# Nine of layer 1's 24 copies of the sample caches, issued at the ends of the two layers' expert sums instead of in layer 1's front

## What is computed

```python
def layer(x, caches, lp):
    q, k, v, zb, gb, u, vc = _mixer_front(_rms(x, g_mix), w_in, q_g, k_g, cv_g)
    ...
    # the sample group also returns its caches, moved on by the 4 new rows
    kv_all = jnp.concatenate([kv_buf, kv_new], axis=1)
    ...
    new_buf = kv_all[:, -lb:]
    h = x + _merge_out(ya, yb, yc, w_out)
    y = h + _peer(_rms(h, g_ffn), pq, pk1, pk2, pu, pv)

def _peer(xn, wq, k1, k2, eu, ev):     # 8 heads, the 16 best of 16384 experts for each
    ...
    hid = gelu(einsum('nd,nhkd->nhk', xb, eu[e]))
    return einsum('nhk,nhkd->nd', g * hid, ev[e])
```

## Time and profile before

| | us |
|---|---|
| median of 3 runs | 1838.96 |
| their range | 1836.76 to 1841.14 |
| the profiled execution | 1838.76 |
| its span | 1836.3 |

### The profile page before, as it was taken

One profiled execution on the slowest core, in us unless ns is written; L12 is line 12 of the kernel. 1 busy time (PEld: TensorE's weight loads), 2 busy tenths in 40 slices (PEclk: granted clock), 3 DMA queues, 4 the chain that ended last, 5 costly groups with the idle time before them and its releaser, 6 DMA issues.

```text
span 1836.3 us, 18530 instructions
## 1 busy us (share of the span) xinstructions
PE 1564.4 (85%) x5844; PEld 841.4 (46%) x5844; DVE 1104.7 (60%) x2779; ACT 606.9 (33%) x1876; POOL 695.3 (38%) x672
## 2 busy tenths in 40 slices
PE   7999999998787887688689998999888877877776
PEld 5789745444343333233157895545433333322221
DVE  2444575777878774454535466566778678644544
ACT  2342433333344332222333334333333333322222
POOL 4020343445444444333313013435454444433341
PEclk8999999999998989999899999999989988999999
DMA  8899899999999999999979988999999999999996
GB/s 280 331 360 365 333 422 421 422 421 421 421 422 421 422 421 421 422 421 421 422 285 371 373 347 355 421 422 421 421 422 421 421 422 421 421 421 422 422 422 274
DMA packets 102490, 729.70 MB, mean 397 GB/s; under 512 B 14828, under 2 KB 15959, under 8 KB 21625
## 3 DMA queue, kind: packets, MB, share of 16 engines
q0 software_dynamic: 90112, 627.43, 82.6%
q1 hardware_dynamic: 11732, 100.48, 14.0%
q10 hardware_dynamic: 548, 0.62, 0.1%
HBM read 724.22 MB, written 48.10 MB: 421 GB/s over the span
## 4 chain that ended last, share of the span: by engine, by line
DMA 45%; PE 38%; DVE 9%; ACT 2%; issue 2%; DVEq 1%; POOL 1%; ACTq 1%; SPq 0%; POOLq 0%
DMA arena<-peer_uv,idx 24%; PE bank L1742 17%; DMA qf<-peer_uv,idx 12%; PE bank L1497 7%; DMA wring<-peer_uv,idx 4%; PE bank L1666 3%; DVE arena L1322 3%; PE bank L1706 2%; DMA yt<-peer_uv,idx 2%; DMA wring<-w_out 1%; PE bank L1492 1%; DVE qf L1322 1%; DVE wring L1322 1%; ACT diag L853 1%; POOL arena L638 1%
## 5 line engine op out<-in xcount | busy, mean ns | idle before, releaser
L1742 PE MATMUL bank<-arena,diag 128*128 128x512 f32 (+1 forms) x1416 | 679.2, 623 | 141.8 <-ACT diag L853 141.8
L638 POOL DMA_INDIRECT arena<-peer_uv,idx x378 | 414.0, 1095 | 651.0 <-PE bank L1742 498.7
L1322 DVE SCALAR_TENSOR_TENSOR arena<-arena,xn 128x1024 f32<-128x1024 f32 x378 | 458.0, 1224 | 324.6 <-DMA arena<-peer_uv,idx 323.1
L1742 PEld LDWEIGHTS bank<-arena,diag 128*128 128x128 f32 (+1 forms) x1416 | 261.6, 192 | 509.4 <-issue 287.8
L845 ACT ACTIVATE act<-hid 128x2 f32<-128x2 f32 x288 | 58.6, 204 | 907.6 <-DVE arena L1322 564.4
L853 ACT ACTIVATE diag<-ident,weight 128x128 f32<-128x128 f32 (+1 forms) x576 | 194.7, 385 | 20.1 <-issue 0.3
L1742 PE MATMUL bank<-wring,diag 128*128 128x512 f32 x328 | 158.5, 617 | 31.6 <-ACT diag L853 31.6
L1742 PE MATMUL bank<-qf,diag 128*128 128x512 f32 (+1 forms) x228 | 119.1, 661 | 41.1 <-ACT diag L853 41.1
L848 ACT ACTIVATE weight<-act,gate 128x1 f32<-128x1 f32 x576 | 138.6, 287 | 21.0 <-issue 1.4
L1322 DVE SCALAR_TENSOR_TENSOR wring<-wring,xn 128x1024 f32<-128x1024 f32 x82 | 100.1, 1226 | 70.2 <-DMA wring<-peer_uv,idx 69.6
L638 POOL DMA_INDIRECT wring<-peer_uv,idx x82 | 92.9, 1133 | 110.0 <-PE bank L1742 99.7
(11 more groups left out here) (286 smaller groups left out, 1587.4 us busy)
## 6 DMA issues: line engine op xcount, KB each, us to landing
kvs<-cache_a_kv_w SPq DMA_DIRECT2D x32, 1022.0 KB, 10.8
wring<-w_col SPq DMA_DIRECT2D x15, 1024.0 KB, 8.3
wring<-w_tok SPq DMA_DIRECT2D x8, 1408.0 KB, 9.0
arena<-peer_wq SPq DMA_DIRECT2D x10, 1024.0 KB, 12.9
kvs<-cache_a_kv_w SPq DMA_DIRECT2D x16, 508.0 KB, 11.8
arena<-peer_uv,idx POOLq DMA_INDIRECT x378, 20.7
qf<-cache_keys POOLq DMA_DIRECT2D x8, 576.0 KB, 11.2
qf<-cache_values POOLq DMA_DIRECT2D x8, 576.0 KB, 21.4
```

Of the source, the lines that this page charges most:

```text
L638: pool.indirect_dma_start(out=ring[j], out_offset=None, in_=io["peer_uv"], in_offset=bass.IndirectOffsetOnAxis(ap=idx[:, n:n + 1], axis=0) ...
L1322: last = v.scalar_tensor_tensor(out=ring[j][:, 0:D], in0=ring[j][:, 0:D], scalar=1.0, in1=xn[:, i, :], op0=ALU.mult, op1=ALU.mult, accum_o ...
L1742: last = pe.matmul(bank[b0 + half][0:r, :], diag[:, n % 16, 0:r], ring[SLOT_OF[n]][:, D + 512 * half:D + 512 * half + 512], start=False, s ...
```

## The change

In layer 1, copies 0 to 4 (six DMAs) leave the loop over chunks and are issued before it, after a wait until `v_used` shows that all but five of layer 0's columns are finished. Copies 20 to 23 (six DMAs) leave their place ahead of the query weights, and are issued ahead of the wait for the last y tile, after a wait until all but five of layer 1's columns are finished. Layer 0's copies stay.

```diff
+EDGE = 5
...
                 if l:
                     sp.wait_ge(xs_ps, 6 * (l - 1) + 4)
                     sp.dma_start(w_home(l, HELD), io["w_col"][l, CHUNKS[HELD][0]]).then_inc(held_loaded, 16)
+                    sp.wait_ge(v_used, COLS * l - 5)
+                    for m in range(EDGE):
+                        shift(l, m)
                 for c in range(2, N_IN + 1):
...
                     for m in range(3 * (c - 2) // 2, 3 * (c - 1) // 2 if c < N_IN else 17):
-                        shift(l, m)
+                        if not l or m >= EDGE:
+                            shift(l, m)
...
                 load_q(l, 1)
-                for m in range(20, 24):
-                    shift(l, m)
+                if l + 1 < DEPTH:
+                    for m in range(20, 24):
+                        shift(l, m)
                 for chunk in (2, 4, 5):
                     load_q(l, chunk)
...
             for i in range(TILES):
+                if i == 2:
+                    sp.wait_ge(v_used, COLS * DEPTH - 5)
+                    for m in range(20, 24):
+                        shift(DEPTH - 1, m)
                 sp.wait_ge(x_done, 3 * (DEPTH - 1) + i + 1)
```

## The result

| | before | after |
|---|---|---|
| median, us | 1839.65 (4 runs, 1836.76 to 1841.14) | 1851.82 (4 runs, 1849.11 to 1854.21) |
| ratio | | 1.0066, interval 1.0051 to 1.0081 |
| the profiled execution, us | 1838.76 (span 1836.3) | 1849.11 (span 1846.7) |

The kernel is slower by 12.2 us. The prediction said 1845.6 and a range up to 1850.0, so the sign is right and the size is not. A later comparison of the same two kernels, with 12 and 35 runs, gave 1846.79 against 1838.14: 8.65 us, ratio 1.0047 (1.0034 to 1.0061). The two intervals, +9.4 to +14.9 and +6.2 to +11.2 us, overlap. The larger sample is the better size of the change, and the 6.8 us of the prediction lie within its interval.

A forecast was written before the change was run, and what follows sets the result against it. The lagging DMA engine at both layers' ends was taken to bound the kernel, its delay passing on one for one. -2.4 + 4.8 - 1.2 + 3.9 + 1.7 = +6.8 us gave 1845.6 us, range 1836.0 to 1850.0.

The forecast's parts named there:

- Part 1: Layer 0's gather: without copy 0's packets the last gather lands earlier, at 935.5 us; -2.4 us.
- Part 2: Layer 0's end: copies 0 to 4, issued after 283 columns, delay the lagging engine's last gather; +4.8 us, bounds 0 and 11.1.
- 2 x 2.4: Layer 0's end: three gather packets and a completion let two 64 KB copy packets pass, 2.4 us each, 4.8 us.
- Rival C: Both layers' ends: all copies pass before the last gather packet; +17.0 us, 1855.8; chance 0.08.
- B: Rival, both layers' ends: copies fall behind the last gather and delay nothing; -3.6 us, 1835.2; chance 0.09.
- Part 3: Layer 1's front: with copies 1 to 4 gone, the 1.2 us wait for w_tok goes; -1.2 us.
- The **0** for copies 20 to 23: Layer 1's front: moving these copies out gains nothing, since the gather waits for VectorE; bounds 0 and -8.0 us.
- Part 4: Layer 1's end: copies 20 to 23, issued after 283 columns, delay the last gather; +3.9 us, bounds 0 and 7.8.
- rival A: Both ends: copies start 0.5 us later, only a part interleaves, clock holds; +2.7 us, 1841.5 in one case; chance 0.33.
- three or two left: Layer 1's end: with three or two gather packets left, copies taking 0.3 + 1.2 = 1.5 us pass.
- Part 5: Both layers' last pairs: longer idling may lower TensorE's clock; +1.7 us, bounds 0 and 3.3.
- I charge half of each: Last pairs: half of a clock drop's cost, 1.5 us in layer 0 and up to 1.8 in layer 1, is charged.

## Why the prediction was right in sign and wrong in size

**What bounds the kernel: right.** Each of the kernels that differ at the layers' ends moved its last dot by what passes the lagging engine (in the one with small packets a late completion comes on top), and leaving out 3.4 MB in the front moved nothing that the runs can tell.

**Part 1, copy 0, -2.4: right.** 2.4 us in the distance to the last dot, and 3.3 and 2.8 us in the medians of the two kernels that did little else. What the part left out is that copy 0's wait also costs clock, 0.6 us on average; the prediction shows the pair after 4.05 us of idling, but uses it only to price the clock.

**Part 2, five copies, +4.8: the mechanism right, the size 6.0.** The order on the engine came as written, 64 KB, completion, 64 KB, completion, from 3.83 us after the issue. The term "2 x 2.4" is what failed. 2.4 us was read off copy 0 while the other engines carried the gather; now all 16 engines copied, and the two packets took 2.78 and 2.81 us, the three gather packets together 0.4 us more than their usual 0.31 each. Rival C, everything ahead, 11.1, did not come. Nor did B: had the eight gather packets gone undivided, the last dot would have kept its step of 2.5 us. The Trainium skill (DMA: Bandwidth & Descriptors, Queues, rings and completion order) lets an engine drain a packet of some 9 to 17 descriptors before it changes queue; the trace disagrees, with one 8 KB row of the gather between two transfers of SP's queue.

**Part 3, the front, -1.2: wrong by most of it.** The step "that is more than the wait of 1.2 us, which goes" failed. w_tok still waited 0.6 us and w_out 0.5, together 1.1 where it was 1.5 (in the repeat of the change 0.6 for w_tok and none for w_out); the kernel with copies 0 and 4 moved away kept 1.3 of 1.5. The copies that stay, and the keys and values on GpSimd's queue, fill the same engines, so a load that loses one copy ahead of it does not land earlier by that copy's whole price. That reading fits the waits, but no run tests it alone. The **0** for copies 20 to 23, with its bound of -8.0, was right within what leaving them out can tell.

**Part 4, four copies at the end, +3.9: 2.0.** I took the copies to start 3.8 us after the issue, with four gather packets left, and charged 0.3 + 1.2 + 2.4. In all four profiles they start 4.07 to 4.09 us after it, with three left, so one 1022 KB copy fewer passes. That is the part's own case "three or two left", 1.5: the packets let pass took 0.30 and 1.27 us, the gather packets 0.06 more, and VectorE started 0.3 to 0.4 us longer after the completion than with no copies, 1.9 to 2.0 in all. The 3.8 us were read at layer 0's end and were 0.3 us short here, which is one gather packet; rival A, copies that start later, is what happened in this layer. "Their own landing costs nothing" held in the changed kernel: the last copy landed at 1841.2, 14.4 us after the first issue, and y was issued at 1844.36. But 1826.3 + 7.8 = 1834.1, with packets priced at 2.4 us, was 1.6 us early. At 286 columns, where y is issued 6 us after the copies, the landing costs 5.1 us.

**Part 5, the clock, +1.7: 4.6 in the first profile, 3.4 in the repeat's.** This is the term with the largest error, and the step that put the forecast and the top of the range too low. Two things failed. "Up to 1.8 in layer 1 (half clock on 3.6 us)" is a slip of arithmetic: work of 3.6 us at half clock costs 3.6 more, not 1.8, and 2.9 were measured. And "I charge half of each" was wrong for layer 0, where all the profiles with 7 us and more of idling have the last pair at 1.06 us a matmul, +1.7. In layer 1, where the idling is 3.2 to 3.3 us, it fell over the first seven of the pair's eight matmuls once (the seventh in part), over its first half once, and once not at all; what decides it is not shown.

**The sum.** With the measured terms it is -2.4 + 6.0 - 0.4 + 2.0 + 1.7 and 0 to 2.9 for layer 1's clock: +6.9 to +9.8 us. The 0.6 us that copy 0 cost in clock come off it. The median of the 12 runs, +8.65, lies in it either way. That the forecast of +6.8 is near is in part luck: part 4 was 1.9 us too high, where parts 2, 3 and 5 were 1.2, 0.8 and up to 2.9 too low. The +12.2 of the first four runs has 2 to 5 us that no part of the change explains. In its profile the first, fourth and fifth stretches add +0.2 net, so the rest is not found there; it may be the small sample, and that stays open.

**The range** ended at 1850.0. The measured terms at their most, +9.8, give 1848.6, inside it, and so does the repeat; the median of the first four runs lies 1.8 us outside. An upper end worked out with the right price of the clock (1.5 + 3.6 instead of 1.7 in the sum) would have started from 1849.0 for the forecast alone, and with 1.2 more for part 2 passed 1850. The range was too narrow by that slip.

## What to carry to other kernels

Work moved out of a busy stretch into an idle-looking one is free only if nobody there is still waiting for a straggler: a DMA share of 0.06 can be the one engine that everything waits for, and each row that it still has to bring lets one of your packets go first. Before moving anything, leave it out once: had these 3.4 MB been left out first, the answer "nothing" would have shown that a new place has little to win. And price a copy by the rate of copies, and a lowered clock by the full length of the work that runs under it.

## What the runs showed of the hardware

- The queues of one DMA engine alternate by single transfer, whatever its size: between two rows of a gather (8 KB, 0.31 us) one packet of SP's queue goes, 64 KB or a completion of 4 bytes. One copy in the queue costs the last gather 2.6 us; five copies cost 6.0, which is two packets and not five, since three rows and a completion were left.
- One of the 16 engines ends its share of the gather 4.0 us after the next slowest in layer 0 (937.45 and 933.47 us before the change) and 3.1 in layer 1. Copies issued by SP start on it 3.8 to 4.1 us after the issue.
- A 64 KB packet of a copy from DRAM to DRAM took 2.41 to 2.44 us beside the gather, and 2.6 to 3.9 when all engines copied; 3.39 MB then took 11.1 us, 305 GB/s, where the gather runs at 421. In 8 KB packets the same copies held all engines busy at 167 to 209 GB/s; most packets took 0.31 to 1.5 us, one took 2.8.
- After 7.2 to 7.8 us of idling TensorE's granted clock was 0.50 (1.2 GHz) over the last pair in all four profiles that had that wait. With 3.2 to 3.3 us it was 0.50 over most of the pair in one profile, over half of it in a second, and 1.00 in a third. Idle matmuls in the gap held it at 1.00 (2.4 GHz).
- In kernels that don't differ there, the stretch of 727 us from layer 1's first addition to its last columns varies by 3.8 us between executions, and the 930 us before layer 0's last columns by 6. Drops of the clock of 3.5 us at different places are a part of it.
